# A decoder layer in split fp32: a first feed-forward chunk of three quads whose sums VectorE makes, and the fourth quad of the other chunks next to the third

## The reference

```python
def swiglu(h, w_gate, w_up, w_down):
    return (jax.nn.silu(h @ w_gate) * (h @ w_up)) @ w_down
...
        h = rms_norm(x, g_ffn[l])
        x = x + swiglu(h, w_gate[l], w_up[l], w_down[l])
    return rms_norm(x, g_final)
```

## Time and profile before

| what | value |
|---|---|
| median of three runs | 1197.78 us (1197.18 to 1198.03) |
| the profiled execution | 1200.37 us, its span 1198.8 us |
| PE busy | 1181.7 us, 99% of the span |
| PEld, DVE, ACT, POOL busy | 81%, 78%, 58%, 11% |
| granted TensorE clock | 0.998 |
| HBM traffic | 285 GB/s over the span |

### The profile page before, as it was taken

One profiled execution on the slowest core, in us unless ns is written; L12 is line 12 of the kernel. 1 busy time (PEld: TensorE's weight loads), 2 busy tenths in 40 slices (PEclk: granted clock), 3 DMA queues, 4 the chain that ended last, 5 costly groups with the idle time before them and its releaser, 6 DMA issues.

```text
span 1198.8 us, 16866 instructions
## 1 busy us (share of the span) xinstructions
PE 1181.7 (99%) x5385; PEld 976.0 (81%) x5385; DVE 939.6 (78%) x1194; ACT 692.9 (58%) x911; POOL 127.0 (11%) x133
## 2 busy tenths in 40 slices
PE   9999999999999999989999999999999999999997
...
GB/s 342 336 256 252 258 260 250 274 228 285 277 265 277 283 258 300 201 284 252 236 268 250 245 248 270 237 247 217 223 238 218 282 209 210 210 219 175 201 208 140
DMA packets 86716, 296.39 MB, mean 247 GB/s; under 512 B 9936, under 2 KB 10704, under 8 KB 85584
## 3 DMA queue, kind: packets, MB, share of 16 engines
...
HBM read 291.60 MB, written 50.33 MB: 285 GB/s over the span
## 4 chain that ended last, share of the span: by engine, by line
PE 69%; DMA 18%; DVE 7%; issue 4%; ACT 1%; POOL 0%; SPq 0%; POOLq 0%; ACTq 0%; DVEq 0%
PE ps L607 16%; PE ps L609 16%; PE ps L608 16%; DMA tsums<-w_stream 15%; PE ps L850 7%; PE ps L851 7%; PE ps L852 7%; DMA raw<-w_stream 3%; DVE wlo L1777 2%; DVE wlo L1418 1%; PE ps L639 1%; PE ps L646 0%; DVE blo L1453 0%; DVE wsum L1784 0%; PE ps L677 0%
## 5 line engine op out<-in xcount | busy, mean ns | idle before, releaser
L1418 DVE TENSOR_TENSOR wlo<-raw,whi 128x1024 fp32r<-128x1024 f32 x160 | 199.7, 1251 | 117.9 <-ACT whi L1014 117.7
L1274 ACT ACTIVATE whi<-raw 128x1024 fp32r<-128x1024 f32 (+1 forms) x189 | 190.3, 1023 | 110.2 <-DMA raw<-w_stream 54.4
L1014 ACT ACTIVATE whi<-raw 128x1024 fp32r<-128x1024 f32 x160 | 168.5, 1059 | 112.6 <-PE ps L609 86.5
L1777 DVE TENSOR_TENSOR wlo<-raw,whi 128x1024 fp32r<-128x1024 f32 (+1 forms) x189 | 219.0, 1177 | 17.0 <-ACT whi L1274 13.1
L607 PE MATMUL ps<-whi,ahi 128*128 128x512 f32 x512 | 200.8, 392 | 1.9 <-DVE wlo L1777 1.6
L609 PE MATMUL ps<-whi,alo 128*128 128x512 f32 x512 | 199.4, 389 | 0.0
L608 PE MATMUL ps<-wlo,ahi 128*128 128x512 f32 x512 | 199.3, 389 | 0.0
L607 PE MATMUL ps<-whi,bhi 128*128 128x512 f32 x448 | 180.1, 402 | 0.0
L609 PE MATMUL ps<-whi,blo 128*128 128x512 f32 x448 | 175.1, 391 | 0.0
L608 PE MATMUL ps<-wlo,bhi 128*128 128x512 f32 x448 | 174.5, 389 | 0.0
L607 PEld LDWEIGHTS ps<-whi,ahi 128*128 128x128 f32 x512 | 96.1, 188 | 22.9 <-DVE wlo L1777 2.5
...
## 6 DMA issues: line engine op xcount, KB each, us to landing
raw<-w_stream SPq DMA_DIRECT2D x378, 512.0 KB, 4.6
tsums<-w_stream SPq DMA_DIRECT2D x44, 512.0 KB, 6.0
tsums<-w_stream POOLq DMA_DIRECT2D x44, 512.0 KB, 9.0
res<-tsums SPq DMA_DIRECT2D x40, 512.0 KB, 4.7
...
res<-x_in ACTq DMA_DIRECT2D x4, 512.0 KB, 7.8
stage<-mem_in ACTq DMA_DIRECT2D x4, 512.0 KB, 7.3
...
```

The source lines that it names most:

```text
L1014: nc.scalar.activation(tile_pair(whi, j), tile_pair(raw, j), ACT.Copy).then_inc(hi_ready, 1)
L1274: nc.scalar.activation(whi_here, src, ACT.Copy).then_inc(hi_ready, 1)
L1418: vec.tensor_tensor(tile_pair(wlo, j), tile_pair(raw, j), tile_pair(whi, j).bitcast(f32), ALU.subtract).then_inc(lo_ready, 1)
L1777: vec.tensor_tensor(lo_here, src, hi_here.bitcast(f32), ALU.subtract).then_inc(lo_ready, 1)
```

## The change

The first chunk gets tables and functions of its own. It has three quads (`FIRST_AT = (3, 9, 14)`) and ten direct steps in 22 steps, loads all 16 tiles in full, and DVE makes all the weight sums of its quads (`first_split`: four operations of 512 columns a quad, in place of two, and a subtraction of 512 columns in its first step, of 1024 in its second, where it was the other way round). The sign convention is that of the down projection, so the casts go through `part_cast`. The scratch in DRAM shrinks to 40 tiles, for chunks 1 to 10. SP copies 31 of them before the feed-forward block and 9 in chunks 0 to 8. On POOL the additions leave the convolution: eight stand ahead of `root(2)`, eight behind it, eleven behind `root(3)`. The SP queue no longer loads sums for chunk 0, and in front of chunk 1 it waits for the squares of the norm in place of the root. The activation sums of the first three quads are made in one set of operations, and those of the fourth quad, which chunk 1 is the first to need, at positions 15 and 19 of chunk 0. ACT's squares stand at 6 and 8. In chunks 1 to 10 the fourth quad starts at step 16, directly behind the third, and the up step that stood between them stands at step 20. The copy of `p1`, the combination and the silu each stand one step earlier.

```diff
-QUAD_AT = (2, 7, 12, 17)
+QUAD_AT = (2, 7, 12, 16)
...
-UP_STEPS = {16: 4, 21: 5, 22: 6, 23: 7}
-RAW_TILES = ("D0", "D1", "Z0", "H0", "D2", "Z1", "H1", "D3", "Z2", "H2", "D4", "Z3", "H3", "D5", "D6", "D7")
-SPLIT_DONE = {0: 1, 1: 2, 4: 7, 7: 12, 10: 17, 12: 21, 13: 22, 14: 23, 15: 24}
-SUMMED = {2: 1, 3: 2, 5: 3, 6: 4, 8: 5, 9: 6, 11: 7}
-T_LOAD_AT = {0: 0, 4: 1, 7: 2, 10: 3}
+UP_STEPS = {20: 4, 21: 5, 22: 6, 23: 7}
+FIRST_QUADS = 3
+FIRST_AT = (3, 9, 14)
+FIRST_CHUNK = CHUNK_RAW + FIRST_QUADS * (QUAD_PARTS - 2)
+FIRST_GATE = {0: 3, 1: 4, 2: 5, 7: 6, 8: 7}
+FIRST_UP = {13: 3, 18: 4, 19: 5, 20: 6, 21: 7}
+FIRST_SUMS = 3 * FIRST_QUADS
+FIRST_DONE = (1, 2, 3, None, 6, 8, 9, None, 12, 14, None, 17)
+FIRST_SUMMED = {3: 3, 7: 6, 10: 9}
+RAW_TILES = ("D0", "D1", "Z0", "H0", "D2", "Z1", "H1", "D3", "Z2", "H2", "Z3", "H3", "D4", "D5", "D6", "D7")
+SPLIT_DONE = {0: 1, 1: 2, 4: 7, 7: 12, 12: 21, 13: 22, 14: 23, 15: 24}
+SUMMED = {2: 1, 3: 2, 5: 3, 6: 4, 8: 5, 9: 6, 10: 7, 11: 8}
+T_LOAD_AT = {0: 0, 4: 1, 7: 2, 9: 3}
...
+TSUMS = QUADS * (NFC - 1)
+COPY_FROM, COPY_TO = 3, 34
+LATE_COPIES = TSUMS - (COPY_TO - COPY_FROM)
...
+P1_AT, COMBINED, SILU_AT = 18, 20, 22
+FIRST_P1, FIRST_COMBINED, FIRST_SILU = 17, 18, 21
...
+            def load_first():
+
+                for n in range(CHUNK_RAW):
+                    if n < RING:
+                        sp.wait_ge(lo_ready, J_FF + n - RING + 1)
+                    elif FIRST_DONE[n - RING] is None:
...
+                        sp.wait_ge(lo_ready, J_FF + FIRST_DONE[n - RING])
+                    sp.dma_start(tile_pair(raw, n), stream[J_FF + n]).then_inc(w_loaded[n % RING], 16)
...
-            with sp.Fori(COPY_FROM + 1, J_FF // RING - 1) as i:
+            with sp.Fori(COPY_FROM + 1, COPY_TO) as i:
                 load_four(i)
                 copy_tile(i)
-            first_sums()
-            load_four(J_FF // RING - 1)
-            copy_tile(J_FF // RING - 1)
-            load_chunk(0, 0, True)
+            with sp.Fori(COPY_TO, J_FF // RING) as i:
+                load_four(i)
+            load_first()
             sp.wait_ge(res_saved, 16 * len(RES_SAVE_AT))
-            sp.wait_ge(rstd_ready, 4)
+            sp.wait_ge(squares, 4 * TT)
...
-                if j % 3 == 0:
-                    add_weights(m)
-                    m += 1
+            for m in range(m, m + 8):
+                add_weights(m)
             root(2)
-            for m in range(m, TSUMS - LATE_COPIES):
+            for m in range(m + 1, m + 9):
                 add_weights(m)
             root(3)
...
+            def first_quad_part(n, part):
...
+                if part == 0:
+                    done = product(up_banks[0], s_form(3), right, opens, False)
+                if part == 1:
+                    p2 = product(gate_banks[0], a_block(0, 1), right, False, closes)
+                    if closes:
+                        p2.then_inc(tile0_done, 1)
+                    done = product(4, a_block(0, 0), left, opens, closes)
+                if part == 2:
+                    product(5, s_form(0), left, opens, closes)
+                    if opens:
+                        pe.wait_ge(unit_lo, U_FF - 1)
+                    done = product(6, s_form(1), right, opens, closes)
+                if part == 3:
+                    product(7, s_form(2), left, opens, closes)
+                    done = product(gate_banks[1], a_block(1, 1), right, False, closes)
+                done.then_inc(step_used, 1)
...
+                        pe.wait_ge(unit_lo, U_FF - 2)
+                if c == 1 and n == QUADS - 1:
                     pe.wait_ge(s_lo, 2)
                 for part in range(QUAD_PARTS):
...
+            def fourth_forms():
+
+                act.wait_ge(s_made, 2)
+                act.wait_ge(step_used, J_FF + min(FIRST_UP) + 1)
+                nc.scalar.activation(ahi[:, KS * FIRST_QUADS, P:2 * P], asum3[:, 0], ACT.Copy)
+                nc.scalar.activation(s3h[:], asum3[:, 1:QUAD_PARTS], ACT.Copy).then_inc(s_hi, 1)
...
-            for p in range(CHUNK):
+            for p in range(FIRST_CHUNK):
                 chunk_cast(0, p + LEAD)
-                if p in (2, 3):
-                    u = SPG - 4 + p
-                    unit(U_H3 + u, KS * u, C_FFN, ahi)
-                if p == 10:
-                    act_forms(1)
-                if p == 12:
+                if p == 2:
+                    for u in (SPG - 2, SPG - 1):
+                        unit(U_H3 + u, KS * u, C_FFN, ahi)
+                if p == 6:
                     await_out(act, G_FF - 1)
                     token_squares(3, 0, res, junk1[:])
-                if p == 14:
+                if p == 8:
                     token_squares(3, 1, res, junk1[:])
+                if p == 12:
+                    nc.scalar.activation(spark_pair[:, 1:2], ones[:, 0:1], ACT.Silu)
                 if p == 16:
-                    nc.scalar.activation(spark_pair[:, 1:2], ones[:, 0:1], ACT.Silu)
-                if p == P1_AT:
+                    fourth_forms()
+                if p == FIRST_P1:
                     p1_copy(0)
-                if p == SILU_AT:
+                if p == FIRST_SILU:
                     gate(0)
...
+            def fourth_forms():
+
+                dve.wait_ge(unit_hi, U_H3 + QUADS)
+                blocks = (araw[:, FIRST_QUADS, k, t, :] for k in range(KS) for t in range(TT))
+                sum_forms(*blocks, [asum3[:, f] for f in range(QUAD_PARTS)], 1)
...
+            def first_split(v, j, n, part):
...
+                b12, b22 = b12_b22[:, 0:GC], b12_b22[:, GC:KS * GC]
+                src = (b22, b11_b21, b12_b22, wsum[:])[part]
+                dve.wait_ge(hi_ready, v + 1)
+                if part == 0:
+                    hi_here, lo_here = hi_here[:, GC:KS * GC], lo_here[:, GC:KS * GC]
+                    vec.tensor_tensor(b12, b12, b11, ALU.add).then_inc(w_sums, 1)
+                vec.tensor_tensor(lo_here, src, hi_here.bitcast(f32), ALU.subtract).then_inc(lo_ready, 1)
+                if part == 0:
+                    dve.wait_ge(w_sums, 3 * n + 1)
+                    vec.tensor_tensor(b22, b22, b12, ALU.add).then_inc(w_sums, 1)
+                if part == 1:
+                    dve.wait_ge(w_sums, 3 * n + 2)
+                    vec.tensor_tensor(wsum[:, 0:GC], b22, b11, ALU.subtract)
+                    vec.tensor_tensor(wsum[:, GC:KS * GC], b22, b21, ALU.add).then_inc(w_sums, 1)
...
-            for p in range(CHUNK):
+            for p in range(FIRST_CHUNK):
                 if p == 0:
                     add_group(G_FF - 1, J_FF)
                 chunk_split(0, p + LEAD)
                 if p == 0:
-                    s_lows(0)
-                if p == 9:
-                    s_forms(1)
-                if p == 10:
-                    s_lows(1)
-                if p in (3, 5):
-                    u = SPG - 2 + (p - 3) // 2
-                    unit(U_H3 + u, KS * u, C_FFN, ahi, alo)
-                if p == 17:
+                    s_lows()
+                if p == 3:
+                    for u in (SPG - 2, SPG - 1):
+                        unit(U_H3 + u, KS * u, C_FFN, ahi, alo)
+                if p == 15:
                     variance(3)
-                if p == COMBINED:
+                    fourth_forms()
+                if p == FIRST_COMBINED:
                     combine(0)
+                if p == FIRST_COMBINED + 1:
+                    fourth_lows()
             def gated_chunk(c, ci):
 
...
```

237 lines of the change are left out of this document (126 added, 111 removed).

## The result

The changed kernel takes 1202.95 us (median of five, 1201.76 to 1203.73) against 1197.78 us; the ratio is 1.0037, with a 95% interval of 1.0024 to 1.0050, so about 4.4 us (5.2 by the two medians). The forecast was 1195.9 us, its range up to 1199.2. Its profiled execution took 1202.65 us with a span of 1201.1, which stands 2.3 us above that of before (1198.8).

A forecast was written before the change was run, and what follows sets the result against it. PE, busy 99% of the span, was taken as the bound: matmul count and time lost between matmuls. Terms +0.7 - 0.9 - 1.2 - 3.5 + 3.0 = -1.9 us, carried to the median 1197.78, gave 1195.9 us; range 1192.6 to 1199.2.

The forecast's parts named there:

- The two waits in the mixer: PE's waits behind a convolution inverse root and the cross-attention query go as POOL's additions move: -0.9 and -1.2 us.
- the small `crstd` wait: In the mixer, PE's other small wait on an inverse root of the convolution was expected to stay.
- The first chunk, the gate and chunk 1: Around chunks 0 and 1, PE's losses fall from 7.8 to 4.3 us: -3.5 us, bounds -6 and +0.
- the gate: SP's wait ahead of chunk 1's loads: waiting for stores only, it opens at 527 us; before, SP passed at 529.17.
- the three matmuls: Chunk 0 has 183 matmuls against 180, three more: +0.7 us.
- The walk: Stepping through DVE's queue in chunk 0: five places where a subtraction lands after PE asks, 2.7 us lost.
- Chunks 1 to 10: The fourth quad's third subtraction comes late for PE, about 0.3 us a chunk: +3.0 us, bounds 0 and +7.5.
- Case E: Rival: VectorE hands over at listed ends, so adjacent quads cost 0.6 us a chunk: 1198.9 us; chance 0.05.
- A: Rival: adjacent quads cost nothing in the steady chunks: -4.9 us, 1192.9 us; chance 0.20.
- C: Rival: first chunk's tiles land late, 7.4 to 9.2 us, shrinking the 3.5 us gain to 0.5 to 1.5: 1198.4; chance 0.12.
- D: Rival: SP's gate before chunk 1 opens no earlier, the last store landing late, 1.1 us more: 1197.0 us; chance 0.08.
- B: Rival: adjacent quads cost DVE's whole excess at the fourth quad, 0.75 us a chunk, 7.5 in all: 1200.4; chance 0.10.

The follow-up runs named there:

- e1: The kernel before run again unchanged, for a second trace: 1198.62 us, ratio 0.9996.
- e8: The changed kernel with ACT's table load for the silu at position 18 of chunk 0 in place of 12: 1202.90 us, ratio 1.0034.
- e11: e3 with POOL's additions behind the root of the feed-forward's norm held back by waits on VectorE's progress: 1197.07 us, ratio 0.9984.
- e7: e4 with the fifteen additions left for the feed-forward block held back by waits on VectorE's progress, two a chunk from chunk 1: 1194.97 us, ratio 0.9969.
- e9: The kernel before, own POOL order, with the ten additions behind the feed-forward norm's root held back by waits on VectorE's progress: 1196.58 us, ratio 0.9983.
- e2: The kernel before with only the fourth quad moved directly behind the third, in all eleven chunks: 1203.12 us, ratio 1.0030.
- e3: The changed kernel with a direct up step again between third and fourth quad in chunks 1 to 10, new first chunk kept: 1199.26 us, ratio 1.0002.
- e10: The changed kernel with its eleven additions behind the root held back as in e9: 1203.71 us, ratio 1.0046.
- e4: The kernel before with only POOL's additions moved out of the convolution's loop, fifteen left for the feed-forward block: 1211.47 us, ratio 1.0086.
- e13: e7 with the fourth quad directly behind the third in all chunks, without the new first chunk: 1200.52 us, ratio 1.0008.

## Why the prediction was wrong

**The two waits in the mixer, -0.9 and -1.2 us.** The mechanism was right: no `crstd` wait is left, the eighth addition is issued at 412.58 (I had 416), `root(2)` runs at 427.32 (428), and the query's wait is gone. Even the small `crstd` wait that I had kept is gone. The size was wrong. I took it from one execution that was 2.6 us above the median, wrote that difference off as a constant, and carried the sum over to the median. e1 shows that the 2 us of these waits are most of that difference: typically there is about 1 us to win (0.7 to 1.1 in the means above).

**The first chunk, the gate and chunk 1, -3.5 us.** This is the step that failed. With the three matmuls it was a forecast of -2.8 us, and chunks 0 and 1 together measured +1.2 (+0.0 and +1.2), some of it from the adjacent quads in chunk 1. Three things went into it.

First, a base that I used twice. The walk had PE lose 2.7 us and arrive at chunk 1 at 537.2, and the load behind the gate let it start at 537.5. It started at 537.52. But I had let PE begin at 494.84, the old place of the first unit, and credited the mixer's 2.1 us besides. From 492.65 on, PE with 2.7 us of losses would have come at 535.0 and waited 2.5 us there. Whatever is won ahead of this place ends at 537: e1 starts chunk 1 at 537.25, the changed kernel at 537.52, e8, with 0.7 us less lost, at 536.98. The forecast's own number forbade the forecast's gain: chunk 0 to 1 could not be 48.5 us. With the 2.1 us counted once, this term is -1.4 and the whole sum +0.2, or 1198.0 us.

Second, the walk found too few misses, though the places were right. The changed kernel lost 1.03 us at the fourth step of the first quad (0.35 forecast with the restart, the four operations on the units' low halves took 1.57 us ahead of the subtraction), 0.1 in the second quad (0.6), 1.60 at the second step of the third (0.1), 0.85 at the step behind it (0.9) and 0.47 at the direct step (0.75), with 0.1 more at each restart. Of the miss at the third quad, 0.67 us was the table load, which I had not put into the queue (e8). The rest is put down to the tile, whose cast waited 2.79 us for the DMA though it landed in 4.7 us, within what I had assumed; no run made it earlier. These losses were hidden too, behind the same bound: that is why the changed kernel's chunk 0 looks no worse than before. With the bound gone, the new first chunk takes 50.2 us (e11) and the old one 47.5 (e7). By that pair it costs 2.7 us, 0.7 of them for the three matmuls, in place of winning 2.8.

Third, the gate. It opened at 528.01 for me (527 forecast), against 526.65 in e1 with the old condition. In e1 the root decided: POOL ended it at 526.19, and the last store, issued at 519.08, had landed at 524.13. In the changed kernel POOL was done at 525.22, and the last store decided: the new chunk issues it at 522.23, 3.1 us later than in e1, and it landed at 527.64. So the new condition by itself won nothing, and with the later store the gate opened 1.4 us later than in e1. Rows of the changed kernel's SP and ACT, for the earlier trace rows:

```profile
522.23 0.43 SPq L458 DMA_DIRECT2D res_kept<-res  x1
...
528.01 0.35 SPq L470 DMA_DIRECT2D res<-tsums  x1
```

```profile
535.15 1.06 ACT L1329 ACTIVATE whi<-raw 128x1024 fp32r<-128x1024 f32 x1 [5.19 <-DMA raw<-w_stream]
```

The cast came at 535.15, where I had 535.2. That number rested on the 8.2 us between gate and cast in the kernel before, and I did not ask what made them so long. It was the addition that POOL issues right behind `root(3)`, and it was worth as much as the whole gain that I forecast: e9 takes it away and gains 2 us.

**Chunks 1 to 10, +3.0 us.** Right in place, mechanism and size for VectorE's part: 0.30 us at the third step of the fourth quad, where 0.14 + 0.03 + 0.10 was forecast, 42.05 us for an undisturbed chunk, 3.6 us for e2 (with three disturbed ones). Too small for the rest: a late tile in the third or fourth quad now reaches PE. In the changed kernel PE lost 0.54 us at that step in chunk 1 and 1.01 in chunk 2, where the fourth quad's second tile was cast at 607.57 after 1.32 us of waiting for its DMA. By e3 adjacency costs 4.2 us in the changed kernel. Case E, the rule of the Trainium skill on the drain ("VectorE: DVE Perf Modes", "The DRAIN you can't avoid") taken with listed durations, is out: the undisturbed chunks lost 0.35 us, not 0.6.

**The rivals.** A (no cost of adjacency) is out. C was half right: tiles were late, but in the third quad of chunk 0, in chunk 1 and chunk 2. The one in chunk 0 landed in 4.7 us, no slower than I had assumed, so its price is not that of C's 7.4 to 9.2 us landings. D was near in its place, a gate that gives nothing, but its sign (SP at the gate beyond 529) did not come, and its price was far too small, as the start of chunk 1 held back the gains of all that stood ahead. No case of mine put together a gate that swallows the gains, a first chunk that loses 5 us, and adjacency with late tiles; 1202.95 lies beyond B as well.

Put together against e1's trace, the changed kernel's is 4.9 us longer: 0.2 less up to the first unit, 1.6 more in chunks 0 and 1, 1.2 more in chunk 2, 3.1 in the eight later intervals and 0.9 less behind them. The loss is mostly that of the adjacent quads, as e3 says too; the first chunk is why no gain stands against it.

Some of it stays open. The down projection and what follows it took 233.6 us from the last units in the changed kernel and in e10, against 234.5 in e1 and 235.3 in e7. It does not go with adjacency: e4, which has none, took 233.6, and e13 234.4; no experiment looked into it. And two traces of the kernel before differ by 2.0 us ahead of the first unit.
